# Two moving operands of 256 columns, or one of 512, in the unit products of a hybrid decoder layer

## The reference

```python
q, k, v, u, gate_a, gate_s = jnp.split(h @ w_in, IN_SPLITS, axis=-1)
merged = jax.nn.sigmoid(gate_a) * attn_branch + jax.nn.sigmoid(gate_s) * ssm_branch
x = x + rms_norm(merged @ w_out, norm_mix_post)
h = rms_norm(x, norm_ffn_pre)
f = (jax.nn.silu(h @ w_ffn_gate) * (h @ w_ffn_up)) @ w_ffn_down
```

## Time and profile before

| | |
|---|---|
| median of 3 runs | 2746.64 us (2743.91 to 2747.68) |
| profiled execution, its span | 2745.42 us, 2743.7 us |
| TensorE busy | 2711.2 us, 99% |
| VectorE busy | 1477.2 us, 54% |
| ScalarE busy | 959.1 us, 35% |
| GpSimd busy | 387.4 us, 14% |
| chain that ended last | TensorE 95%, VectorE 2%, DMA 1%, ScalarE 1% |
| HBM traffic | 132 GB/s over the span |

### The profile page before, as it was taken

The page is one execution under the profiler, slowest core; times in us unless marked ns, Lnnn a source line. Parts: engine busy times, 40 slices in busy tenths (PEclk is TensorE's granted clock), DMA queues, the critical chain, the costliest instruction groups (busy, mean ns, idle before and its releaser), DMA issues.

```text
span 2743.7 us, 45116 instructions
## 1 busy us (share of the span) xinstructions
PE 2711.2 (99%) x17837; PEld 2455.4 (89%) x17837; DVE 1477.2 (54%) x1685; ACT 959.1 (35%) x1237; POOL 387.4 (14%) x610
## 2 busy tenths in 40 slices
PE   7999999999999999999999999999999999999998
PEld 6788888888888999988889999999999998888887
DVE  5333332243345788742667777777777763334334
ACT  5222322231422444432533433344333342223223
POOL 5958007761000000000000000000000000000000
PEclk9999999999999999999999999999999999999999
DMA  6443553337433444452424334233333345444443
GB/s 174 145 136 126 127 131 93 100 75 165 150 119 115 170 139 144 168 192 94 152 92 134 113 107 137 99 127 118 107 130 107 127 141 210 140 147 145 142 149 131
DMA packets 261235, 364.78 MB, mean 133 GB/s; under 512 B 23152, under 2 KB 212656, under 8 KB 259600
## 3 DMA queue, kind: packets, MB, share of 16 engines
q1 hardware_dynamic: 232232, 287.89, 32.7%
q0 software_dynamic: 11616, 57.09, 6.9%
q10 hardware_dynamic: 17288, 18.40, 2.0%
HBM read 320.41 MB, written 42.93 MB: 132 GB/s over the span
## 4 chain that ended last, share of the span: by engine, by line
PE 95%; DVE 2%; DMA 1%; ACT 1%; issue 1%; POOL 0%; ACTq 0%; SPq 0%; DVEq 0%
PE ps L653 13%; PE ps L654 13%; PE ps L651 13%; PE ps L437 8%; PE ps L439 8%; PE ps L441 8%; PE ps L689 6%; PE ps L687 6%; PE ps L688 6%; PE ps L537 2%; PE ps L535 2%; PE ps L536 2%; PE ps L516 2%; PE ps L520 2%; PE ps L518 2%
## 5 line engine op out<-in xcount | busy, mean ns | idle before, releaser
L425 DVE TENSOR_TENSOR w_lo<-raw,w_hi 128x1024 fp32r<-128x1024 f32 x180 | 236.8, 1316 | 512.3 <-ACT w_hi L421 511.8
L421 ACT ACTIVATE w_hi<-raw 128x1024 fp32r<-128x1024 f32 x180 | 190.6, 1059 | 561.0 <-PE ps L441 350.3
L437 PE MATMUL ps<-a_hi,w_hi 128*128 128x512 f32 x656 | 258.6, 394 | 1.6 <-issue 1.2
L439 PE MATMUL ps<-a_lo,w_hi 128*128 128x512 f32 x656 | 255.6, 390 | 0.0
L441 PE MATMUL ps<-a_hi,w_lo 128*128 128x512 f32 x656 | 255.4, 389 | 0.0
L653 PE MATMUL ps<-a_lo,w_hi 128*128 128x256 f32 x872 | 246.8, 283 | 0.0
L651 PE MATMUL ps<-a_hi,w_hi 128*128 128x256 f32 x872 | 246.8, 283 | 0.0
L654 PE MATMUL ps<-a_hi,w_lo 128*128 128x256 f32 x872 | 246.8, 283 | 0.0
L664 DVE TENSOR_TENSOR f_lo<-f_raw,f_hi 128x512 fp32r<-128x512 f32 x84 | 58.2, 693 | 260.5 <-ACT f_hi L660 260.5
L654 PE MATMUL ps<-a_hi,w_lo_b 128*128 128x256 f32 x640 | 181.1, 283 | 0.0
L653 PE MATMUL ps<-a_lo,w_hi_b 128*128 128x256 f32 x640 | 181.1, 283 | 0.0
(11 more groups left out here) (405 smaller groups left out, 7736.8 us busy)
## 6 DMA issues: line engine op xcount, KB each, us to landing
raw<-in_w_in SPq DMA_DIRECT2D x124, 512.0 KB, 3.7
raw<-in_w_ffn_gate SPq DMA_DIRECT2D x88, 512.0 KB, 4.6
raw<-in_w_ffn_down SPq DMA_DIRECT2D x88, 512.0 KB, 3.9
raw_b<-in_w_ffn_up SPq DMA_DIRECT2D x80, 512.0 KB, 5.5
f_raw<-f_d SPq DMA_DIRECT2D x88, 256.0 KB, 2.7
raw<-in_w_out SPq DMA_DIRECT2D x32, 512.0 KB, 3.7
mix_raw_b<-in_w_in SPq DMA_DIRECT2D x28, 512.0 KB, 5.2
f_d<-f_t ACTq DMA_DIRECT2D x22, 512.0 KB, 2.8
```

The lines of the kernel that those rows point to most:

```text
L421: nc.scalar.activation(w_hi[:, m % 2, :], raw[:, m % 4, :], ACT.Copy).then_inc(hi_ready, 1)
L425: nc.vector.tensor_tensor(w_lo[:, m % 2, :], raw[:, m % 4, :], w_hi[:, m % 2, :].bitcast(F32), ALU.subtract).then_inc(lo_ready, 1)
L437: nc.tensor.matmul(o, wh[:, k, cols], x_hi[:, kt0 + k, :], start=first and k == 0, stop=False, skip_group_check=halves)
L439: nc.tensor.matmul(o, wh[:, k, cols], x_lo[:, kt0 + k, :], start=False, stop=False, skip_group_check=halves)
```

## The change

The high and the low inputs of a product become two halves of one tensor (`a_both`, `s_both`, `gs_both`). For a product in `x_both` one matmul of 512 moving columns, in two pieces of 256, multiplies the high weights with both and writes both halves of the bank; the third matmul still has 256 columns and adds to the left half. In `FFN` all seven products are in `x_both`, in `MIX` products 1, 3 and 6. The sum is then spread over the two halves of a bank, and whoever reads it must add them:

- Z and W (both units): ScalarE copies the right halves of both banks after product 3 into the output row (`zw_copied`), VectorE adds the left halves (`zw_made`, 512 elements), then `c22` and `c12` come from one add of `q` to the row. Product 6 waits for `zw_made`. `c21` takes two dependent adds (`c21_half`).
- X and Y (`FFN` only): ScalarE copies the right half for `p1` and `c11`, VectorE adds the left half; `u2` and `q` take two dependent adds each (`u2_half`, `q_half`).

The banks are renumbered so that Z and W are neighbours. `Silu` of `c11` joins the later one, now of 512 elements. Waits are renamed from `c12_made` to `zw_made` where needed.

```diff
-        a_hi = at_kb("a_hi", 0, [P, KT, SEQ], F32R)
-        a_lo = at_kb("a_lo", 32, [P, KT, SEQ], F32R)
+        a_both = at_kb("a_both", 0, [P, 2, KT, SEQ], F32R)
+        a_hi, a_lo = (a_both[:, i, :, :] for i in range(2))
...
+                self.x_both = {1: sums_both[0], 3: sums_both[2], 6: a_both[:, :, k2, quad[1]]}
+                if g0:
+                    self.x_both |= {0: a_both[:, :, k1, quad[0]], 2: sums_both[1], 4: a_both[:, :, k1, quad[1]],
+                                    5: a_both[:, :, k2, quad[0]]}
...
         def unit_bank(j, name):
-            return ps[:, 4 * ((j + 1) % 2) + "XZYW".index(name), 0:2 * P]
+            return ps[:, 4 * ((j + 1) % 2) + "XYZW".index(name), 0:2 * P]
+
+        def unit_bank_halves(j, name):
+
+            return ps[:, 4 * ((j + 1) % 2) + "XYZW".index(name), :].rearrange("p (a n) -> p a n", a=2)
+
+        def unit_zw(j, half):
+
+            b = 4 * ((j + 1) % 2)
+            return ps[:, b + 2:b + 4, quad[half]]
+
+        def halves(row):
+            return row.rearrange("p (t n) -> p t n", t=2)
+
+        def both_halves(t):
+            return t.unsqueeze(1).broadcast_to([P, 2, 2 * P])
...
             if p == 6:
-                pe.wait_ge(c22_made, u + START + 1)
+                pe.wait_ge(zw_made, u + START + 1)
             o = unit_bank(j, "XZYWYXW"[p])
...
+            wide = unit_bank_halves(j, "XZYWYXW"[p])
             for k in range(KT // 2):
-                nc.tensor.matmul(o, wh[:, k, :], ph.x_hi[p][:, k, :], start=p < 4 and k == 0, stop=False,
-                                 skip_group_check=True)
-                nc.tensor.matmul(o, wh[:, k, :], ph.x_lo[p][:, k, :], start=False, stop=False, skip_group_check=True)
+                if p in ph.x_both:
+                    nc.tensor.matmul(wide, wh[:, k, :], ph.x_both[p][:, :, k, :], start=p < 4 and k == 0, stop=False,
+                                     skip_group_check=True)
+                else:
+                    nc.tensor.matmul(o, wh[:, k, :], ph.x_hi[p][:, k, :], start=p < 4 and k == 0, stop=False,
+                                     skip_group_check=True)
+                    nc.tensor.matmul(o, wh[:, k, :], ph.x_lo[p][:, k, :], start=False, stop=False,
+                                     skip_group_check=True)
                 mm = nc.tensor.matmul(o, wl[:, k, :], ph.x_hi[p][:, k, :], start=False, stop=k == KT // 2 - 1,
                                       skip_group_check=True)
             mm.then_inc(product, 1)
...
+                if p == 4:
+                    act.wait_ge(product, PROD0 + MIX.times7(g, j) + 4)
+                    if first and j == 0:
+                        act.wait_ge(gl_stored, 16 * 7)
+                    if j >= 2:
+                        act.wait_ge(m_made, 2 * g + 1)
+                    elif not (isinstance(g, int) and g == 0):
+                        act.wait_ge(m_made, 2 * g)
+                    nc.scalar.activation(halves(sg[j % 2][:, 1, :]), unit_zw(j, 1), ACT.Copy).then_inc(zw_copied, 1)
...
                     act.wait_ge(product, PROD0 + FFN.times7(g, j) + 1)
                     act.wait_ge(q_made, START + u)
-                    nc.scalar.activation(p1_s[:, :], unit_bank(j, "X"), ACT.Copy).then_inc(p1_copied, 1)
+                    nc.scalar.activation(p1_s[:, :], unit_bank_halves(j, "X")[:, 1, :], ACT.Copy).then_inc(p1_low, 1)
+                if p == 4:
+                    a = j // 2
+                    act.wait_ge(product, PROD0 + FFN.times7(g, j) + 4)
+                    if j % 2 == 0:
+                        act.wait_ge(f_made, START + 2 * g + a)
+                        row = f_sg[:, 1, :]
+                    else:
+                        act.wait_ge(f_stored[a], START + 16 * g)
+                        row = f_t[:, a, 1, :]
+                    nc.scalar.activation(halves(row), unit_zw(j, 1), ACT.Copy).then_inc(zw_copied, 1)
                 if p == 6:
                     a = j // 2
                     act.wait_ge(product, PROD0 + FFN.times7(g, j) + 6)
                     if j % 2 == 0:
                         act.wait_ge(f_made, START + 2 * g + a)
-                        nc.scalar.activation(f_sg[:, 0, quad[0]], unit_bank(j, "X"), ACT.Silu).then_inc(c11_read, 1)
+                        o = f_sg[:, 0, quad[0]]
                     else:
                         act.wait_ge(f_stored[a], START + 16 * g)
-                        nc.scalar.activation(f_t[:, a, 0, quad[0]], unit_bank(j, "X"), ACT.Copy).then_inc(c11_read, 1)
+                        o = f_t[:, a, 0, quad[0]]
...
             def mix_c21(u, j):
+                o = sg[j % 2][:, 0, quad[1]]
                 dve.wait_ge(product, PROD0 + 7 * u + 7)
-                tt(sg[j % 2][:, 0, quad[1]], MIX.u2[:, :], unit_bank(j, "W"), ALU.add).then_inc(c21_made, 1)
+                tt(o, MIX.u2[:, :], unit_bank(j, "W"), ALU.add).then_inc(c21_half, 1)
+                dve.wait_ge(c21_half, u + 1)
+                tt(o, o, unit_bank_halves(j, "W")[:, 1, :], ALU.add).then_inc(c21_made, 1)
...
                     operand_lo(dve, MIX, g, j, 6)
+                    dve.wait_ge(product, PROD0 + MIX.times7(g, j) + 4)
+                    dve.wait_ge(zw_copied, u + 1)
+                    row = halves(sg[j % 2][:, 1, :])
+                    tt(row, row, unit_zw(j, 0), ALU.add).then_inc(zw_made, 1)
...
                     tt(MIX.q[:, :], MIX.p1[:, :], unit_bank(j, "Y"), ALU.add).then_inc(q_made, 1)
                     dve.wait_ge(q_made, START + u + 1)
-                    tt(sg[j % 2][:, 1, quad[1]], MIX.q[:, :], unit_bank(j, "W"), ALU.add).then_inc(c22_made, 1)
+                    dve.wait_ge(zw_made, START + u + 1)
+                    row = halves(sg[j % 2][:, 1, :])
+                    tt(row, row, both_halves(MIX.q[:, :]), ALU.add).then_inc(c22_made, 1)
...
                 if p == 6:
-                    tt(sg[j % 2][:, 1, quad[0]], MIX.q[:, :], unit_bank(j, "Z"), ALU.add).then_inc(c12_made, 1)
...
             def c21(g, j):
+                u, o = FFN.at(g, j), unit_out(j, 0, 1)
                 dve.wait_ge(product, PROD0 + FFN.times7(g, j) + 7)
-                tt(unit_out(j, 0, 1), u2_s[:, :], unit_bank(j, "W"), ALU.add).then_inc(c21_made, 1)
+                tt(o, u2_s[:, :], unit_bank(j, "W"), ALU.add).then_inc(c21_half, 1)
+                dve.wait_ge(c21_half, u + 1)
+                tt(o, o, unit_bank_halves(j, "W")[:, 1, :], ALU.add).then_inc(c21_made, 1)
...
                 if p == 2:
+                    dve.wait_ge(p1_low, u - MIX_UNITS + 1)
+                    tt(p1_s[:, :], p1_s[:, :], unit_bank(j, "X"), ALU.add).then_inc(p1_copied, 1)
...
                     dve.wait_ge(product, PROD0 + FFN.times7(g, j) + 3)
                     dve.wait_ge(p1_copied, START + u + 1)
-                    tt(u2_s[:, :], p1_s[:, :], unit_bank(j, "Y"), ALU.add).then_inc(u2_made, 1)
+                    tt(u2_s[:, :], p1_s[:, :], unit_bank(j, "Y"), ALU.add).then_inc(u2_half, 1)
+                    dve.wait_ge(u2_half, u - MIX_UNITS + 1)
+                    tt(u2_s[:, :], u2_s[:, :], unit_bank_halves(j, "Y")[:, 1, :], ALU.add).then_inc(u2_made, 1)
...
                 if p == 4:
                     operand_lo(dve, FFN, g, j, 6)
+                    dve.wait_ge(product, PROD0 + FFN.times7(g, j) + 4)
+                    dve.wait_ge(zw_copied, u + 1)
+                    row = halves(unit_row(j, 1))
+                    tt(row, row, unit_zw(j, 0), ALU.add).then_inc(zw_made, 1)
...
                 if p == 5:
                     dve.wait_ge(product, PROD0 + FFN.times7(g, j) + 5)
-                    tt(q_s[:, :], p1_s[:, :], unit_bank(j, "Y"), ALU.add).then_inc(q_made, 1)
+                    tt(q_s[:, :], p1_s[:, :], unit_bank(j, "Y"), ALU.add).then_inc(q_half, 1)
+                    dve.wait_ge(q_half, u - MIX_UNITS + 1)
+                    tt(q_s[:, :], q_s[:, :], unit_bank_halves(j, "Y")[:, 1, :], ALU.add).then_inc(q_made, 1)
                     dve.wait_ge(q_made, START + u + 1)
-                    if j % 2:
-                        dve.wait_ge(f_stored[j // 2], START + 16 * g)
-                    tt(unit_out(j, 1, 1), q_s[:, :], unit_bank(j, "W"), ALU.add).then_inc(c22_made, 1)
+                    dve.wait_ge(zw_made, START + u + 1)
+                    row = halves(unit_row(j, 1))
+                    tt(row, row, both_halves(q_s[:, :]), ALU.add).then_inc(c22_made, 1)
...
                 if p == 6:
-                    tt(unit_out(j, 1, 0), q_s[:, :], unit_bank(j, "Z"), ALU.add).then_inc(c12_made, 1)
...
                         down_lo(dve, 1, 0)
+                    dve.wait_ge(c11_low, u - MIX_UNITS + 1)
+                    o = unit_out(j, 0, 0)
+                    tt(o, o, unit_bank(j, "X"), ALU.add).then_inc(c11_read, 1)
```

More of the change, by code:

```diff
@@ L184, in build @@
         s_tmp = at_kb("s_tmp", 100, [P, 4, KT // 2, 2 * P])
-        s_hi = at_kb("s_hi", 132, [P, 3, KT // 2, 2 * P], F32R)
-        s_lo = at_kb("s_lo", 156, [P, 3, KT // 2, 2 * P], F32R)
```

(25 more changed lines are left out.)

24 lines of the change are left out of this document (12 added, 12 removed).

## The result

| | before | after |
|---|---|---|
| median of 5 runs | 2746.64 us (2743.91 to 2749.59) | 2761.05 us (2759.44 to 2763.23) |
| profiled execution, its span | 2745.42 us, 2743.7 us | 2760.40 us, 2758.7 us |
| TensorE, VectorE, ScalarE busy | 99%, 54%, 35% | 98%, 57%, 36% |
| matmuls | 17837 | 15261 |

The ratio is 1.0053, with a 95% interval of 1.0040 to 1.0066: slower by 14.4 us, where 13.3 us were forecast. TensorE issues 2576 matmuls fewer, and the kernel takes longer.

What follows compares the result with a forecast made beforehand. TensorE bounds the kernel now; after the change VectorE would pace the FFN units. FFN +17.0, MIX -4.5 and down projection start +0.8 sum to +13.3 us on the profiled 2745.42, forecast 2760 us from the median, range 2735 to 2776.

Steps and rivals of the forecast that it cites:

- VectorE's own loop: VectorE's work per FFN unit before the change, its stays for ScalarE included: 17.51 us, against TensorE's 20.16 us.
- 3.14 us: Work and waits the change adds to VectorE per FFN unit, making its loop 20.65 us against TensorE's new 19.41.
- `block_sum` 2 to `c11`: VectorE, FFN unit: the `c11` add awaits ScalarE's copy, 1.36 us after the high part starts; +0.61 us with its slot.
- Low part 6 to `zw`: VectorE: `zw` awaits ScalarE's copy, ready at 2.55 us with low part 6 starting at 1.09; +0.92 us per unit.
- Dependent adds: VectorE, FFN unit: `u2`, `q` and `c21` each become two dependent adds, 3 x 0.45 = +1.35 us.
- start of the down projection: After the last FFN unit: VectorE comes out late and delays the first low parts, +0.8 us, an estimate.
- the lead that VectorE could lose once: FFN stage: VectorE can fall behind by 2.6 us before TensorE stops, once; subtracted to reach +17.0 us.
- the price of the wide matmul: TensorE: a 512-column matmul in two pieces takes 226.7 ns, saving 13.3 ns per k; MIX units 19.84 us, -4.5 us.
- a wide matmul spaced by other than 226.7 ns: Sign named in advance, in the profile of TensorE's matmuls, that the prediction is wrong.
- The other half of the MIX forecast: MIX units: VectorE gains 1.29 us to 19.88, level with TensorE's 19.84; TensorE still paces.
- The first: Rival, FFN units: VectorE keeps ahead, TensorE paces at 19.41 us, 2712 us; additions at most 1.90 us; chance 0.12.
- The fourth: Rival, FFN units: VectorE and TensorE wait for each other; 5 us more, 2765, or above 2776, the latter 0.06.
- The fifth: Rival: the two-piece wide matmul takes 240 ns and gains nothing; MIX loses its 4.5 us, 2764 us; no separate chance.

Runs made afterwards that it cites:

- e1: Changed kernel with ScalarE's copy for `c11` in the FFN units moved ahead of the step 6 high part; 2736.84 us, ratio to before 0.9966.
- e2: e1 plus ScalarE's Z and W copy ahead of high part 3 and VectorE's `zw` add ahead of low part 6; 2728.86 us, again 2729.18 us.
- e6: Changed kernel without the second, dependent adds of `u2`, `q` and `c21` in the FFN units, output not the layer's; 2729.79 us, ratio to before 0.9937.
- e5: Changed kernel with the wide matmul split back into two of 256 columns in both units, all adds and copies kept; 2763.16 us, ratio to before 1.0061.
- e9: e2 with FFN products 2 and 4 (bank Y) back to narrow matmuls, `u2` and `q` one add each; 2734.49 us, ratio to before 0.9952.
- e10: e2 with each product's 8 wide matmuls issued first and its 8 narrow ones behind them, in both units; 2719.73 us, ratio to before 0.9900.

## Why the prediction was right, and where it was off

**The limit changed hands, as forecast.** The step that carried the forecast was that VectorE's own loop is 17.51 us and not the busy share, and that 3.14 us come on top. Measured: 20.60 us per unit against 20.65 forecast. The trace confirms it by the wait for `u2` that is gone, the new rows of waits and the timeline; e1, e2 and e6 confirm it by taking away parts of the 3.14 us, e5 by making TensorE slower at no cost.

**Term by term.** `block_sum` 2 to `c11`: 1.22 + 0.12 + 1.36 = 2.70 us follow from the same rows, 2.69 measured. Low part 6 to `zw`: 2.55 - 1.09 = 1.46 expected, 1.50 measured. ScalarE's copy of 512 elements from two banks: 0.577 us where 0.60 was taken from a `Square`. The 512-wide `c22`: 0.61 us to the next start (1588.87 to 1589.48) for 0.60. Dependent adds: 0.45 us each (1575.86 to 1576.31). Where nothing is awaited the next operation still starts before the previous one ends: 0.69 us of duration and 0.61 us to the next start. The rule of the Trainium skill ("VectorE: DVE Perf Modes", section "The DRAIN you can't avoid"), by which 10 us more would have been due, is again not borne out by these rows. The prediction left out that the same passage goes on to say that a next operation which is not held starts earlier, which is what the rows show where nothing is awaited.

**FFN units and start of the down projection:** +17.0 + 0.8 forecast, +16.5 measured up to the first matmul of the down projection, nothing after it. Two terms were mis-sized. From the last `u2` to that matmul it takes 10.72 us, and 11.32 before, so the 0.8 us did not come. And the lead that VectorE could lose once was put at 2.6 us, the mean of all units. With the measured loop of 20.60 us this gives 40 x 20.60 - 806.4 - 2.6 = 15.0 us. The stage begins with less, as VectorE's wait before the first `u2` shows, before and after the change:

```profile
1458.36 0.42 DVE L2188 TENSOR_TENSOR u_s<-p_s,ps 128x256 f32<-128x256 f32 x1 [0.99 <-PE ps L654]
1456.73 0.42 DVE L2255 TENSOR_TENSOR u_s<-p_s,ps 128x256 f32<-128x256 f32 x1 [0.54 <-PE ps L688]
```

Without any lead the formula gives 40 x 20.60 - 806.4 = 17.6 us; 17.6 - 16.5 = 1.1 us is the lead that was used. That it is the 0.99 us of the first unit is read off these rows and was not tried.

**MIX units: the step that failed is the price of the wide matmul.** The prediction took 226.7 ns from rows in which 512-wide matmuls follow one another, and got -4.5 us. Alternating with narrow ones, a pair takes 353.3 ns here, and -2.1 us came out: 20.0 us per unit for the 19.84 forecast. The prediction had named a wide matmul spaced by other than 226.7 ns as a sign that it is wrong, and here that sign came true. The trace gives 6.7 ns saved per pair in the MIX units, 13.3 ns in the quick stretches. By the rule of the Trainium skill ("TensorE: Matmul & The Clock Gate", section "Back-to-back issue gap"), which the page gives for an isolated matmul, it would have been 2.5 ns and -0.8 us, which these rows don't bear out either. The total hardly shows the error, since the FFN units, where it would have weighed nearly seven times as much, were hidden behind VectorE. There the prediction was right for the reason given; in the slower executions of a kernel like e2 it would have been 15 us wrong. The other half of the MIX forecast, VectorE level with TensorE, came out: VectorE's waits before the `u2` of these units fell from 20.9 to 3.0 us in the 14 units.

**The closeness of the total is partly luck.** Between the spans 15.0 us were measured where 13.3 were forecast: 1.3 less than forecast in the FFN units and the start of the down projection, 2.4 more in the MIX units, and 0.6 ahead of them that no term had.

**Rivals.** The first, at 2712 us, is what e2 nearly reached in its quick executions (2714 to 2717 us) once the additions had been brought under the 1.90 us that it asked for. The fourth, engines that wait for each other, didn't occur: the unit stayed at VectorE's own sum. The fifth, a wide matmul of 240 ns, is half true: with the narrow one at 120 ns, a pair of 353.3 ns leaves it 233.3. TensorE's idle time was put at 1.2 us per FFN unit and came out at 0.56 in its waits. The granted clock was 1.00 in the stretches with gaps, as assumed.

## What to carry to other kernels

Compare an engine's own loop, stays included, with the pace of the limiting engine; the lead before its one long wait (here 2.65 us of a 20.16 us unit) is what a change may spend, not the idle share. When work is added to an engine, look for the stays that it already has: two adds put into existing waits cost nothing. Behind those waits the first cost 0.6 us per unit (e1) and the second at least 0.56 (e2, where TensorE then set the pace); 1.53 was the forecast for both. If the copy that feeds such an add waits for nothing more than the instruction in front of it does, it belongs ahead of that one in its queue.

## What the runs showed of the hardware

**A pair of a 512- and a 256-column matmul has two durations**, 346.7 and 353.3 ns, at a granted clock of 1.00 and without any wait. Both are averages over a repeated pattern of starts. The shorter one repeats after two pairs, 231 + 112 and 233 + 117 ns (e2 at 1600 us); the longer one after three, 232 + 118, 240 + 120 and 236 + 114 ns (e9 at 1901 us). MIX units showed the longer one throughout, in all traces with alternating widths; FFN units began with it and went over to the shorter one after 10 us (e2, e6), went back 50 us later (e6), or kept the longer one throughout (e9). In the changed kernel and in e1, where TensorE has gaps, both occur by turns. Twelve executions of e2 gave three times near 2715 and nine near 2729 us. Matmuls of one width in a row had one spacing, 120.0 or 226.7 ns, in the kernel before; in e10 eight wide ones that follow narrow ones took 1.84 us, 230 ns each. What decides between the two stays open; that it hangs on the alternation is supported by the one cluster of e10, and was not taken further.

**Handing over between ScalarE and VectorE** costs 0.03 us towards VectorE and 0.12 us towards ScalarE (1590.10 + 1.22 against 1591.44). Two such round trips per unit are 2 x 0.15 = 0.3 us that no busy share shows.
